# Hybrid attention and mixture-of-experts block: rows of four experts picked and turned in one product

## The reference: what is computed

```python
def hierarchical_moe(h, w_rg, b_rg, w_re, b_re, w_gate, w_up, w_down):
    T = h.shape[0]
    lg = jnp.dot(h, w_rg, preferred_element_type=jnp.float32) + b_rg      # 4 groups
    pg = jax.nn.softmax(lg, axis=-1)
    _, g_top = lax.top_k(lg, 1)
    ...
    top_p, top_i = lax.top_k(jax.nn.softmax(le_g, axis=-1), TOP_K)        # 2 of the group's 8 experts
    weights = p_grp * top_p
    experts = (g_top * EXP_PER_GROUP + top_i).astype(jnp.int32)
    return expert_dispatch(h, experts, weights, w_gate, w_up, w_down)

def run_block(args):            # for each of 32 experts, on the rows sent to it
    xb, e = args
    return (jax.nn.silu(xb @ w_gate[e]) * (xb @ w_up[e])) @ w_down[e]
```

## Time and profile before

| what | value |
|---|---|
| median of 3 runs | 2007.7 us (2003.36 to 2011.37) |
| the profiled execution | 2007.3 us, its span 2005.2 us |
| PE busy | 1765.2 us (88% of the span) |
| DVE, ACT, POOL busy | 705.2 us (35%), 520.9 us (26%), 154.0 us (8%) |
| DMA | 550.54 MB, mean 275 GB/s |
| gate and up weights | 256 transfers of 1024.0 KB, 20.4 us from issue to landing |
| down weights | 128 transfers of 1024.0 KB, 21.1 us |
| chain that ended last | PE 64%, DMA 16%, DVE 8%, SP's queue 4%, ACT 4%, issue 3% |

### The profile page before, as it was taken

The page is one execution under the profiler, slowest core; times in us unless marked ns, Lnnn a source line. Parts: engine busy times, 40 slices in busy tenths (PEclk is TensorE's granted clock), DMA queues, the critical chain, the costliest instruction groups (busy, mean ns, idle before and its releaser), DMA issues.

```text
span 2005.2 us, 26541 instructions
## 1 busy us (share of the span) xinstructions
PE 1765.2 (88%) x9249; PEld 1001.7 (50%) x9250; DVE 705.2 (35%) x1476; ACT 520.9 (26%) x1061; POOL 154.0 (8%) x190
## 2 busy tenths in 40 slices
PE   4999899989977999989999599989868999888884
PEld 2766566668743443334333487778723333222223
DVE  4465355444553111111112664673531111111113
ACT  4344444442331111001111554451311111011011
POOL 0063031000000000000000234310000000000000
PEclk8999999999988999999999699999979999999996
DMA  8346555323255999999999343334488999999993
GB/s 316 132 169 230 193 201 212 109 69 93 97 217 210 422 420 421 421 421 395 409 420 420 124 137 90 108 100 145 142 339 304 421 420 421 421 420 421 420 421 131
DMA packets 96047, 550.54 MB, mean 275 GB/s; under 512 B 14162, under 2 KB 15650, under 8 KB 42724
## 3 DMA queue, kind: packets, MB, share of 16 engines
q1 hardware_dynamic: 83108, 526.89, 66.7%
q0 software_dynamic: 4224, 11.35, 2.0%
q10 hardware_dynamic: 8640, 11.28, 1.6%
HBM read 537.15 MB, written 12.32 MB: 274 GB/s over the span
## 4 chain that ended last, share of the span: by engine, by line
PE 64%; DMA 16%; DVE 8%; SPq 4%; ACT 4%; issue 3%; POOL 0%; ACTq 0%; POOLq 0%; DVEq 0%
PE ps L779 14%; DMA moe<-in_w_exp_gate_up_dram 13%; PE ps L493 8%; PE ps L495 8%; PE ps L494 8%; PE ps L795 8%; PE ps L760 4%; SPq L412 3%; PE ps L712 2%; PE ps L639 2%; PE ps L668 2%; PE ps L650 2%; DMA moe<-in_w_mod_dram 1%; DVE w_lo L1297 1%; SPq L417 1%
## 5 line engine op out<-in xcount | busy, mean ns | idle before, releaser
L779 PE MATMUL ps<-moe,ht 128*64 128x512 f32 x2048 | 474.6, 605 | 61.4 <-DMA moe<-in_w_exp_gate_up_dram 42.6
L779 PEld LDWEIGHTS ps<-moe,ht 128*64 128x64 f32 x2048 | 141.8, 138 | 383.4 <-issue 264.8
L1653 DVE TENSOR_TENSOR arena<-aux,ps 128x256 f32<-128x256 f32 x64 | 26.9, 421 | 678.1 <-ACT aux L1197 678.1
L493 PE MATMUL ps<-ht_hi,w_hi 128*128 128x512 f32 (+1 forms) x704 | 253.1, 359 | 3.0 <-ACT arena L1084 1.6
L495 PE MATMUL ps<-ht_hi,w_lo 128*128 128x512 f32 (+1 forms) x704 | 244.3, 347 | 0.0
L494 PE MATMUL ps<-ht_lo,w_hi 128*128 128x512 f32 (+1 forms) x704 | 244.1, 347 | 0.0
L795 PE MATMUL ps<-moe,arena 128*64 128x512 f32 x1024 | 233.8, 599 | 2.5
L1297 DVE TENSOR_TENSOR w_lo<-ws,w_hi 128x1024 fp32r<-128x1024 f32 (+1 forms) x122 | 148.5, 1222 | 223.5 <-ACT w_hi L989 223.5
L989 ACT ACTIVATE w_hi<-ws 128x1024 fp32r<-128x1024 f32 (+1 forms) x122 | 125.2, 1026 | 176.6 <-PE ps L495 147.1
L493 PEld LDWEIGHTS ps<-ht_hi,w_hi 128*128 128x128 f32 x704 | 134.0, 190 | 25.6 <-issue 9.3
L495 PEld LDWEIGHTS ps<-ht_hi,w_lo 128*128 128x128 f32 x704 | 133.7, 190 | 16.8
(11 more groups left out here) (253 smaller groups left out, 2143.3 us busy)
## 6 DMA issues: line engine op xcount, KB each, us to landing
moe<-in_w_exp_gate_up_dram SPq DMA_DIRECT2D x256, 1024.0 KB, 20.4
moe<-in_w_exp_down_dram SPq DMA_DIRECT2D x128, 1024.0 KB, 21.1
ws<-in_w_in_dram SPq DMA_DIRECT2D x92, 512.0 KB, 4.1
moe<-in_w_mod_dram SPq DMA_DIRECT2D x29, 1536.0 KB, 6.6
y_rows<-arena ACTq DMA_DIRECT2D x164, 64.0 KB, 5.5
ws<-in_w_branch_dram SPq DMA_DIRECT2D x16, 512.0 KB, 3.5
ws<-in_w_out_dram SPq DMA_DIRECT2D x16, 512.0 KB, 3.5
arena<-in_w_mod_dram SPq DMA_DIRECT2D x3, 1536.0 KB, 20.1
```

The source lines that it names most:

```text
L493: pe.matmul(ps[:, bank, 0:cols], w[:, k, :], a_hi, start=(i == 0), stop=False)
L779: mm = pe.matmul(ps[BLK * j:BLK * j + BLK, 2, :].rearrange("p (g n) -> p g n", g=2), xg[:, k, BLK * s:BLK * s + BLK], w[k // 2][:, k % 2, ...
```

## The change

The mask covers four experts (256 columns for each token tile), and the product is turned round: a 128-column chunk of the tokens' rows is the stationary side and the mask is the moving side, so that the picked rows come out transposed at once, one chunk of the width for four experts. The transposes of the rows and the buffer `xs` go. There are 8 chunks, two in a bank, the two banks in turn. The PE loop goes over 8 fours with four experts written out; each expert runs two chunks for the next four. The next rows are held in a new buffer `xg_next` (three quarters of them); in every fourth expert DVE copies them to `xg` and the last quarter straight from PSUM. Only the first expert of four waits for `xg`, now chunk pair by chunk pair within `gate_up`.

The overflow code on PE stands once for each expert, in a loop of two rounds with an inner loop (one pass, then the rest). ACT's and DVE's overflow code stays as it is. DVE does the arithmetic of `dest` and `route_w` between the first mask and the copies of the first rows. ACT no longer waits for it before the first expert. Some small buffers have other places.

```diff
-AHEAD = 4
+FOUR = 4
+AHEAD = 2 * FOUR
 PAIRS = NE // 2
+QUADS = NE // FOUR
...
-        xg, xs = part(ht_flat, 8, 4, KC, P), part(ht_flat, 12, 4)
+        xg, xg_next = part(ht_flat, 8, 8, KC, FOUR * BLK), part(ht_flat, 0, 6, KC - 2, FOUR * BLK)
...
-        pick = placed("pick", [P, 4, 2 * BLK], ARENA_AT + 38 * 1024, F32R)
-        ysb, ysb_o = part(arena, 40, 2), part(arena, 42, 1)
+        pick = placed("pick", [P, 4, FOUR * BLK], ARENA_AT + 38 * 1024, F32R)
+        ysb, ysb_o = part(arena, 42, 2), part(arena, 45, 1)
...
-        act_g, act_g_o = aux[:, 0, 0:256], aux[:, 1, 0:P]
+        act_g, act_g_o = part(arena, 32, 1), aux[:, 1, 0:P]
...
-                def pick_x(half):
+                def gather(chunk):
+                    bank, at = 7 * (chunk // 2 % 2), FOUR * BLK * (chunk % 2)
                     for tile in range(nt):
                         for rows in (hr_hi, hr_lo):
-                            mm = pe.matmul(ps[:, 7 * half, :], pick[:, tile, :], rows[:, tile, 512 * half:512 * half + 512],
+                            mm = pe.matmul(ps[:, bank, at:at + FOUR * BLK], rows[:, tile, chunk * P:(chunk + 1) * P], pick[:, tile, :],
                                            start=(tile == 0 and rows is hr_hi), stop=(tile == nt - 1 and rows is hr_lo))
-                    if half:
-                        mm.then_inc(g["xs_done"].sem, 1)
-                def turn_x(half):
-                    for c in range(4):
-                        at = (4 * half + c) * P
-                        mm = pe.transpose(ps[:, 7 * half, c * P:(c + 1) * P], xs[:, at:at + P], ident[:, :])
-                    if half:
-                        mm.then_inc(g["xt_done"].sem, 1)
-                def gate_up(s, slot, landed):
+                    if chunk % 2:
+                        mm.then_inc(g["xg_done"].sem, 1)
+                def gate_up(s, slot, landed, turned):
 
...
                             pe.wait_ge(gu_in[slot][k // 2].sem, landed * 16)
+                            if s == 0:
+                                pe.wait_ge(g["xg_set"].sem, turned + k // 2 + 1)
...
-                pair0, pick0 = (PAIRS + 1) * l, (PAIRS + 2) * l
+                gathered, pick0 = 4 * (QUADS + 1) * l, (QUADS + 2) * l
                 pe.wait_ge(g["pick_set"].sem, pick0 + 1)
-                pick_x(0)
-                pick_x(1)
-                pe.wait_ge(g["xs_copied"].sem, pair0 + 1)
-                turn_x(0)
-                turn_x(1)
-                def expert(e, two, s):
-                    done, landed, slot = NE * l + e, PAIRS * l + two + 1, s
+                for chunk in range(KC):
+                    if chunk in (4, 6):
+                        pe.wait_ge(g["xg_set"].sem, gathered + chunk // 2 - 1)
+                    gather(chunk)
+                def expert(e, four, s):
+                    done, slot = NE * l + e, s % 2
+                    landed = PAIRS * l + 2 * four + s // 2 + 1
                     n = pe.value_load(n_of[0:1, bass.ds(e, 1)], min_val=0, max_val=NTOK)
-                    pe.wait_ge(g["xt_copied"].sem, pair0 + two + 1)
                     pe.nop(nofuse=True)
                     with pe.If(n > BLK):
                         if s:
-                            pe.wait_ge(g["xs_copied"].sem, pair0 + two + 2)
-                        def more_block(b):
-                            more_slots(pe.snap(n_more, min_val=0, max_val=64), slot, landed, s, two)
-                            pe.reg_add(n_more, n_more, 1)
-                        more_block(BLK // MORE)
-                        with pe.If(n > BLK + MORE):
-                            with pe.Fori(BLK // MORE + 1, w_all // MORE) as b:
-                                with pe.If(n > b * MORE):
-                                    more_block(b)
+                            pe.wait_ge(g["xg_held"].sem, QUADS * FOUR * l + 4 * four + s)
+                        else:
+                            pe.wait_ge(g["xg_set"].sem, gathered + 4 * four + 4)
+                        pe.nop(nofuse=True)
+                        with pe.Fori(0, 2) as rest:
+                            with pe.If(n > BLK + MORE * rest):
+                                with pe.Fori(0, 1 + (w_all // MORE - BLK // MORE - 2) * rest) as b:
+                                    with pe.If(n > BLK + MORE * rest + MORE * b):
+                                        more_slots(pe.snap(n_more, min_val=0, max_val=64), slot, landed)
+                                        pe.reg_add(n_more, n_more, 1)
+                                    pe.nop(nofuse=True)
                                 pe.nop(nofuse=True)
+                            pe.nop(nofuse=True)
                         pe.nop(nofuse=True)
                     pe.nop()
-                    gate_up(s, slot, landed)
+                    gate_up(s, slot, landed, gathered + 4 * four)
                     if s == 0:
-                        pe.wait_ge(g["pick_set"].sem, pick0 + two + 2)
+                        pe.wait_ge(g["pick_set"].sem, pick0 + four + 2)
                     else:
-                        pe.wait_ge(g["xs_copied"].sem, pair0 + two + 2)
-                    next_pair = turn_x if s else pick_x
-                    next_pair(0)
+                        pe.wait_ge(g["xg_held"].sem, QUADS * FOUR * l + 4 * four + s)
+                    gather(2 * s)
                     pe.wait_ge(g["hid_done"].sem, done + 1)
                     turn_h(hid)
-                    next_pair(1)
+                    gather(2 * s + 1)
                     pe.wait_ge(g["hidt_copied"].sem, done + 1)
                     pe.wait_ge(g["y_copied"].sem, done + 1)
-                    down(4, hid_t, s, PAIRS * l + two + 1)
-                with pe.Fori(0, PAIRS) as two:
-                    for s in range(2):
-                        expert(2 * two + s, two, s)
+                    down(4, hid_t, slot, landed)
+                with pe.Fori(0, QUADS) as four:
+                    for s in range(FOUR):
+                        expert(FOUR * four + s, four, s)
...
-                act.wait_ge(g["dest_set"].sem, g["dest_set"].at(l, 2))
...
-                def set_pair(e):
-                    out = pick[:, 0:nt, :].rearrange("p t (j n) -> p t j n", j=2)
-                    v.tensor_tensor(out, place1[:, 0:nt, bass.ds(e, 2)].unsqueeze(3).broadcast_to([P, nt, 2, BLK]),
-                                    slots1[:, 0:BLK].unsqueeze(1).unsqueeze(1).broadcast_to([P, nt, 2, BLK]), ALU.is_equal) \
+                def set_four(e):
+                    out = pick[:, 0:nt, :].rearrange("p t (j n) -> p t j n", j=FOUR)
+                    v.tensor_tensor(out, place1[:, 0:nt, bass.ds(e, FOUR)].unsqueeze(3).broadcast_to([P, nt, FOUR, BLK]),
+                                    slots1[:, 0:BLK].unsqueeze(1).unsqueeze(1).broadcast_to([P, nt, FOUR, BLK]), ALU.is_equal) \
                         .then_inc(g["pick_set"].sem, 1)
...
-                def copy_xs():
-                    v.tensor_copy(xs[:, 0:512], ps[:, 0, :])
-                    v.tensor_copy(xs[:, 512:1024], ps[:, 7, :]).then_inc(g["xs_copied"].sem, 1)
-                def copy_xg():
-                    v.tensor_copy(xg[:, 0:4, :], ps[:, 0, :].rearrange("p (k n) -> p k n", n=P))
-                    v.tensor_copy(xg[:, 4:8, :], ps[:, 7, :].rearrange("p (k n) -> p k n", n=P)).then_inc(g["xt_copied"].sem, 1)
-                pair0 = (PAIRS + 1) * l
-                set_pair(0)
-                dve.wait_ge(g["xs_done"].sem, pair0 + 1)
-                copy_xs()
-                set_pair(2)
-                dve.wait_ge(g["xt_done"].sem, pair0 + 1)
-                copy_xg()
+                def gathered_rows(p):
+                    return ps[:, 7 * (p % 2), :].rearrange("p (k n) -> p k n", n=FOUR * BLK)
+                done0 = 4 * (QUADS + 1) * l
+                def first_rows(p):
+                    dve.wait_ge(g["xg_done"].sem, done0 + p + 1)
+                    v.tensor_copy(xg[:, 2 * p:2 * p + 2, :], gathered_rows(p)).then_inc(g["xg_set"].sem, 1)
+                set_four(0)
                 for k in range(2):
...
+                first_rows(0)
+                first_rows(1)
...
+                first_rows(2)
+                first_rows(3)
+                set_four(FOUR)
...
-                    if s == 0:
-                        dve.wait_ge(g["xs_done"].sem, pair0 + two + 2)
-                        copy_xs()
-                    else:
-                        dve.wait_ge(g["xt_done"].sem, pair0 + two + 2)
-                        copy_xg()
-                        set_pair(e + 3)
-                with dve.Fori(0, PAIRS) as two:
-                    for s in range(2):
-                        expert(2 * two + s, two, s)
+                    if s < 3:
+                        dve.wait_ge(g["xg_done"].sem, done0 + 4 * four + s + 5)
+                        v.tensor_copy(xg_next[:, 2 * s:2 * s + 2, :], gathered_rows(s)).then_inc(g["xg_held"].sem, 1)
+                        return
```

(18 more changed lines are left out.)

## The result

The changed kernel took 2071.7 us (median of 4 runs, 2067.9 to 2075.1) where the kernel before, beside it, took 2006.0 (2003.4 to 2011.4): ratio 1.032, 95% interval 1.029 to 1.035. Forecast were 1984.9 us and a range of 1977 to 2002, with a chance of 0.08 for slower.

A forecast was written before the change was run, and what follows sets the result against it. Weight transfers, not PE, bound the kernel, so only the time they stand still counts. Gains of 4.2 + 6.7 + 2.7 + 1.2 + 7.6 = 22.4 us off 2007.3 gave 1984.9 us; range 1977 to 2002.

The forecast's parts named there:

- Is the code still held?: Layer 0's PE loop: about 1650 instructions for some 1290, put at no cost, though no row showed that it stays.
- that rival: Layer 0's loop no longer held, each expert waiting 4.6 us for code: 68 us, 2053 in all; chance 0.08.
- Start, layer 0: First mask to first weight reload in layer 0: about 14.5 us, the reload at 621.9 against 626.12, 4.2 us sooner.
- Start, layer 1: First mask to first weight reload in layer 1: the reload at 1478.5 against 1485.23, 6.7 us sooner.
- The 1.5 us for code ahead of gate-up: PE's wait from the last pick product to the first gate-up, taken as 1.5 us between bounds 0 and 5.53.
- Stall at the start of layer 0: Transfers standing still after layer 0's start: 3.8 us before, 2.7 us gained.
- Second overflow there: Stall after layer 0's second overflow, 4.5 us before: three experts at 12.8 us instead of 39.6 together, 1.2 us gained.
- Layer 1's first stall: Transfers standing still at layer 1's start, through expert 2's overflow: 8.2 us instead of 15.8, 7.6 gained.
- Steady state: Experts between stalls: PE at 12.8 us (layer 0) and 12.4 (layer 1), under DMA's 15.2, so nothing gained.
- The three extra copies of every fourth expert: DVE's copies of the next picked rows, hidden behind down products: nothing; uncovered, 0.5 us every four experts.
- The route arithmetic: DVE's 16 small operations moved ahead of the first copies: hidden beside the picks; at most 4 us if uncovered.
- Rivals 1 and 3: 1: PE still waits for code before first gate-up, 1996.5, chance 0.20. 3: no effect, within 5 us of 2007, 0.10.

The follow-up runs named there:

- the kernel with its code held: The changed kernel with 48 small products in an unused bank behind layer 0's last router product, moving the loop's start; 1982.8 us, ratio 0.988 to the kernel before.
- the short one: The changed kernel with PE's overflow code left out for the third and fourth of each four experts in layer 0; 1981.4 us, ratio 0.987 to the kernel before.

## Why the prediction was wrong

**The step that failed is "Is the code still held?".** It saw the danger, its length (1650 instructions by its count from the source, 1636 in the program) and the "eight or nine lines of eight", and then gave the case in which it costs much 0.08. Two things went wrong there. It argued that the loop before ran with no block fetched and took the new one to stay by default, although that row held for a loop in six blocks and said nothing of eight. And its argument against, that "the shorter jump of about as many mostly lands in the very next one", is about jumps inside the round. It is true as far as it goes (the stops there are 1.8 and 3.5 us), but says nothing of the way back to the top: once eight blocks are touched and one is fetched ahead, nine in all, the top is gone each time it is wanted, and then so is every block after it. The 9 fetches a round say just that: every block of the loop and the one ahead, each time.

The Trainium skill, Runtime: NRT & Kernel Launch, section Instruction fetch mechanics, has a store of 2048 instructions for PE, filled in order, so eight blocks of 256. The traces agree with it: seven touched blocks stay, 2 fetches in 435 us, both in the first 12, and eight don't, 54 in 445. The Trainium skill's Advanced Engine Details and Errata, section ISA Cache, says "Only 2 cache lines!"; here they disagree: the loop before touches six blocks and fetched none. With the block ahead counted in, the first of these two rules gives the loss for a loop that touches eight. Whether a loop touches seven or eight depends on where it starts, which the prediction did not count; and the count made afterwards is off by some 50 instructions, so it would have called two of the quick kernels slow.

**The price** in that rival was 4.6 us an expert, from layer 1's expert 1, and 2053 us as a whole. Measured, from the mask of layer 0 to the start of its last down products 1181.71 - 609.37 = 572.3 us, and in the kernel with its code held 1090.98 - 609.46 = 481.5. The first is now PE's own time: the third and fourth rounds take 66.6 and 66.9 (755.92 to 822.51 to 889.41) where 4 x 12.8 = 51.2 are work, so 3.9 us an expert, a little under 4.6. The two rounds with an overflow take 168.8 together (889.41 to 1058.19), 35 more than two of those; before, the overflows lay mostly under the transfers, and they lie in the open once PE is the bound. The rival left them out, and counted the slack against 15.2 us an expert, where the kernel with its code held needs (481.5 - 11) / 32 = 14.7. So 91 us in the place of 68.

**With the code held the sum was right.** It gave 1984.9; the kernels whose loop is held take 1981.4 and 1982.8. Term by term, by the kernel with its code held:
- Start, layer 0: reload 13.2 us after the mask (622.61 less 609.46); forecast 14.5. In the changed kernel itself it is 623.83 less 609.37, 14.5. Picks of 256 columns take 0.21 us apart at the lower clock until 615.1 and 0.12 thereafter, as forecast.
- Start, layer 1: 9.0 (1469.19 less 1460.22; in the changed kernel 1557.15 less 1547.94, 9.2); forecast 10.1. The 1.5 us for code ahead of gate-up, taken between two bounds, was too much.
- Stall at the start of layer 0: 31 x (1 - 403/421) = 1.3 us instead of 3.8; forecast 1.1. The 0.5 us that it gave to the first byte isn't there: in the kernel before the stretch begins at 627.0 and the first packet of weights starts at 627.1.
- Second overflow there: 35 x (1 - 411/421) = 0.8 instead of 4.5. Mis-sized: 3.7 gained where 1.2 was put, since PE arrives at it without lag.
- Layer 1's first stall: 60 x (1 - 353/421) = 9.7 instead of 15.8; forecast 8.2. Mis-sized by 1.5 the other way, but not by the change: the small products shift layer 1's code too, and there expert 1 waits 1.8 us and a later one of the first four 1.4 us at "issue". The three unshifted kernels (the changed one, the short one and the one with the route arithmetic last) have no such wait there; in the short one the stall is 59 x (1 - 358/421) = 8.8.
- Steady state: 421 GB/s and nothing gained, as forecast. The three extra copies of every fourth expert show nowhere.
- The route arithmetic: forecast as hidden, at most 4 us if uncovered. Its place makes no difference that the runs can tell (1981.4 and 1983.2).

From mask to mask layer 0 came out at 850.8 us, 10.2 less than before, forecast 8.1; from the second mask to the end 523.3, 13.5 less, forecast 14.3; unshifted it is 15.3 to 16.0 less, shifted 11.8 to 13.5. The sum came out closer than its terms: the second overflow gave 2.5 us more than forecast and, with the shift, layer 1's stall 1.5 less. And the first mask comes 0.2 to 2.1 us later in these kernels' profiles than in that of before, ahead of anything that the diff touches, so a us or two of a single profile is drift.

**Rivals 1 and 3** didn't come about: gate-up of layer 0 in the changed kernel starts at 620.51 without the wait of 5.53 us, and the start's gains are there in full. The kernel with the shorter overflow loop alone shows that this wait was for code indeed: shorter code removed it.

What stays open: the exact rule by which blocks go (eight places filled in turn fits all runs, with an offset that was only inferred). The length of a wait is clearer. At the way back of the changed kernel two packets start within the 9.0 us, at 675.4 and 681.7, and PE goes on 2.7 us after the second; at the start of layer 0 in the kernel before one starts within the 5.53 us, at 619.8, and PE goes on 2.5 us after it. The first was under full load (415 GB/s from 675.4 to 684.3) and the second with the weights' queue idle, so these two show no price of the load; that was not tried by itself. Why the two packets stand 6.2 us apart, where others follow in 3.1, isn't shown.

## What to carry to other kernels

Count the instructions of a loop's body in blocks of 256, where it begins and ends and with the block fetched ahead, before you unroll or lay more branches into it; a body that touches eight, with the one ahead nine, lost every one of them each round here. If the count comes within some 60 instructions of a boundary, run it shifted as well. In a profile the sign is the instruction queue: packets in a steady loop, with "issue" ahead of PE at the way back. It is cured by shorter code, or by a few instructions ahead of the loop that move it over the boundary, put where the engine waits anyway.

## What the runs showed of the chip

- PE holds a loop that touches seven blocks of 256 instructions, with one fetched ahead; one that touches eight has 9 fetches a round and 8.8 to 9.4 us of idle PE at its way back (up to 10.8 with layer 1 padded). Which blocks a loop touches rests on a count with an inferred offset of 48 to 65 instructions.
- The step is sharp: two kernels that differ in 32 instructions ahead of the loop, 85 us apart.
- Code that a single jump steps over cost nothing until it was entered (no fetch from 655 to 860 us with 1786 instructions in the loop, 2025.9 us in all); the same amount in branches side by side costs 418 us.
- A wait already met isn't free on PE: 200 of them took between 9.6 us (the part in the open) and 14.4 us (all of PE's idle time around them).
- After a stop of 3.3 to 9.4 us the granted clock is at the lower of its levels for a while (0.50 from 684.4 to 688.0), and 32 gate-up products take 8.7 to 10.5 us instead of 7.04. The slow clock, 0.90 on average in layer 0, is thus part of the price of a fetch.
